# A product with the output matrix in three rounded float32 products, and four expert slots filled later

## The chip, the core and the metric

One core of one Trainium2 chip runs the whole block in one launch. The metric is the device time of an execution in microseconds; lower is better. The profile is one execution, taken by the hardware profiler. Its engines are called TensorE (PE, with weight loads as PEld), VectorE (DVE), ScalarE (ACT), GpSimd (POOL) and SyncE (SP). SyncE only issues DMAs here.

## What is computed

One layer of a streaming encoder over 512 tokens of width 1024, all in float32:

```python
h = layernorm(x, ln0)
q, k, v, z, xbc, dt, g = split(h @ w_in)
ya = window_attention(q, k, v, sinks) @ w_out_attn
ys = ssd(xbc, z, dt, ...) @ w_out_ssd
mix = (sigmoid(gA) * ya + sigmoid(gS) * ys) @ w_out     # the product that is changed
h1 = layernorm(alpha * h + mix, ln1)
moe = hier_moe(h1)        # 32 experts, d_ff 256: one of 4 groups, top 2 of its 8 experts
ple = sigmoid(h1 @ w_ple_gate + b) * (p @ w_ple)
out = layernorm(alpha * h1 + moe + ple, ln2)
```

## The kernel before

The program is written engine by engine, with hand-placed semaphores; each engine runs its own list in order. SBUF is one arena whose regions change hands. Its head is a ring of 12 slots of 2048 words in each partition (1.05 MB for the 128), into which SyncE loads the weight matrices in a fixed order, and which later holds the expert weights: a pair of experts takes six slots (gate, up and down for each half), pair 0 slots 0 to 5, pair 1 slots 6 to 11, pair 2 slots 0 to 5 again, and so on. `MOE_FREED` names, for each slot, the semaphore and the value that SyncE waits for before it loads an expert matrix there the first time.

TensorE multiplies plain fp32 operands slowly. Where it matters, the kernel splits both operands into a part rounded to fp32r (`hi`) and the rest (`lo`), and adds three products, `hi*hi + hi*lo + lo*hi` (helper `thrice`, line 875). ScalarE makes a `hi` by a copy (L1327), VectorE or GpSimd the `lo` by a subtraction (L737, L1895, L1908). The input projection and the product with `w_out_ssd` are done so. The products with `w_out_attn` (L1084), with `w_out` (L1103) and all later ones are plain fp32: one such matmul shows as two instructions in the trace.

The stretch around the change, in order:

1. `ya`: 8 output blocks of 128 columns, transposed (columns in partitions, tokens in the free dimension), into 8 PSUM banks. VectorE multiplies each with its gate into `mixT` (L1904).
2. `ys` (L875 in this stretch): 8 output blocks of 24 products each. VectorE gates a block out of PSUM (L1916, `s_ys_read`) and adds it to `mixT` (L1920, `s_mix_ready`).
3. The product with `w_out` (L1103): tokens are now in the partitions. For each of 4 token tiles and 2 halves of 512 columns, 8 matmuls over the contraction blocks go to one bank. It starts when all 8 blocks of `mixT` are there. `w_out` lies in slots 0, 1, 8, 9.
4. VectorE, for each token tile: two additions to the residual (L1929) and a layer norm (L1607 to L1613), which gives h1 (`s_h1_ready`). It also needs the rows of ln1, which GpSimd's queue loads after `ys` (L777). SyncE stores each tile of h1 to DRAM (L655, L660).
5. TensorE transposes p (L1110) and h1 (L1126) and multiplies h1 with the router (L1118). VectorE turns the logits into ranks and rows. Between, TensorE makes the first PLE gate products (L1152, L1155), which need the gate slices (four column quarters of `w_ple_gate`) and `w_ple`.
6. The first rows are gathered by GpSimd's queue, transposed (L1171), and the experts run in 16 pairs: gate and up (L1214), transposes (L1239), down (L1229). SyncE refills a pair's gate and up slots when its gate/up product is done (`s_gu_mm`), its down slots after the down product.

SyncE's list in this stretch: it waits for `ya`, loads gate slice 1, then slots 2 to 5 and 6, 7 as the `ys` product frees them; then gate slice 0, slots 10 and 11; the rows of h1 for tiles 0 to 2; after the output product `w_ple`, slots 0 and 1; the rows of tile 3; slots 8 and 9; gate slices 2 and 3 when h1 is stored and transposed.

## Time and profile before

| | |
|---|---|
| median of 3 runs | 800.39 us (799.8 to 800.94) |
| the profiled execution | 799.58 us, of it 797.8 us in the span |
| TensorE busy | 737.4 us, 92% of the span |
| VectorE, ScalarE, GpSimd busy | 406.7, 188.7, 163.0 us |
| DMA | 173.14 MB, mean 217 GB/s |

All times of the trace count from the start of the span. The page gives busy times of the engines, their course in 40 slices of 19.9 us, the chain of work that ended last, and the costliest groups of instructions. A matmul's record is longer than the step from one to the next, since matmuls are pipelined: the step is read from the starts of two instructions, or from the chain.

### The profile page before, as it was taken

To read this page: it belongs to the slowest core of one execution; us is meant where nothing else is said; L and a number is where in the kernel's file an instruction comes from. 1 tells how busy PE (TensorE), PEld (TensorE's weight loads), DVE (VectorE), ACT (ScalarE), POOL (GpSimd) and SP (SyncE) were. 2 spreads that over 40 slices of the span, in tenths; PEclk is the share of its full clock that TensorE was granted. 3 is DMA by queue.
4 is the path that set the end of the run, shared out by engine and by line. 5 is a ranking of instruction groups with operands and counts; after the bars stand their busy time and mean duration, and the time that the engine had idled before them with its cause. 6 is when DMAs were issued, how large, how long until landed. Compare 5 with 4: busy or idle time off the path is not lost.

```text
span 797.8 us, 9564 instructions
## 1 busy us (share of the span) xinstructions
PE 737.4 (92%) x3735; PEld 499.3 (63%) x3735; DVE 406.7 (51%) x743; ACT 188.7 (24%) x335; POOL 163.0 (20%) x121
## 2 busy tenths in 40 slices
PE   4999999999999999999999999999999989888672
PEld 2898788998887888747854488544554444444220
DVE  5598946775678888563216558411212021111317
ACT  3312424555322223240000060211121121111121
POOL 4924490000032222000000001411111111111242
PEclk9999999999999999999999999999999999999985
DMA  9798132311111122424268174499999999999492
GB/s 312 257 408 199 53 106 60 101 53 53 50 58 53 53 53 54 148 90 158 106 249 331 53 288 134 132 406 419 408 413 418 417 423 419 421 421 421 173 203 108
DMA packets 61815, 173.14 MB, mean 217 GB/s; under 512 B 16982, under 2 KB 39712, under 8 KB 47946
## 3 DMA queue, kind: packets, MB, share of 16 engines
q1 hardware_dynamic: 52324, 141.79, 47.1%
q0 software_dynamic: 8752, 28.59, 11.0%
q10 hardware_dynamic: 694, 2.14, 0.7%
q8 instruction: 31, 0.51, 0.3%
q14 instruction: 14, 0.11, 0.0%
HBM read 155.52 MB, written 24.67 MB: 226 GB/s over the span
## 4 chain that ended last, share of the span: by engine, by line
PE 72%; DMA 15%; DVE 8%; issue 2%; POOL 1%; ACT 1%; SPq 0%; POOLq 0%; DVEq 0%
PE psum L875 31%; PE psum L1214 10%; PE psum L1103 7%; DMA ring<-in_w_exp_up_dram 6%; PE psum L1229 5%; PE psum L1152 4%; PE psum L1084 3%; DMA ring<-in_w_in_dram 3%; DMA arena<-y_rows,rowsU 2%; PE psum L1033 2%; PE psum L1053 1%; DMA info<-row_info 1%; PE psum L983 1%; PE psum L1171 1%; PE psum L952 1%
## 5 line engine op out<-in xcount | busy, mean ns | idle before, releaser
L875 PE MATMUL psum<-ring_r 128*128 128x512 f32 (+1 forms) x832 | 215.4, 346 | 3.1 <-DVE arena_r L1638 1.7
L875 PEld LDWEIGHTS psum<-ring_r 128*128 128x128 f32 x832 | 146.2, 193 | 24.3 <-issue 3.0
L875 PE MATMUL psum<-arena_r,ring_r 128*128 128x512 f32 (+1 forms) x416 | 141.4, 377 | 0.0
L1327 ACT COPY arena<-psum 128x512 f32<-128x512 f32 (+4 forms) x104 | 57.1, 580 | 264.6 <-PE psum L1110 110.6
L1214 PE MATMUL psum<-ring,arena 128*64 128x512 f32 x512 | 112.9, 593 | 4.7 <-DMA ring<-in_w_exp_up_dram 4.7
L737 POOL TENSOR_TENSOR ring_r<-ring,ring_r 128x2048 fp32r<-128x2048 f32 x16 | 73.9, 4621 | 205.0 <-ACT ring_r L1327 205.0
L875 PEld LDWEIGHTS psum<-arena_r,ring_r 128*128 128x128 f32 x416 | 79.7, 192 | 13.7 <-issue 0.5
L1214 PEld LDWEIGHTS psum<-ring,arena 128*64 128x64 f32 x512 | 39.5, 137 | 75.4 <-issue 75.4
L1229 PE MATMUL psum<-ring,arena 128*64 128x512 f32 x256 | 61.3, 622 | 8.3 <-issue 8.3
L1152 PE MATMUL psum<-arena 128*128 128x256 f32 x256 | 63.0, 392 | 1.1 <-DVE rowsU L2061 1.1
L2092 DVE SCALAR_TENSOR_TENSOR arena<-arena,psum 128x256 f32<-128x256 f32 x16 | 9.7, 607 | 104.3 <-ACT arena L1515 104.3
L1152 PEld LDWEIGHTS psum<-arena 128*128 128x128 f32 x256 | 47.1, 192 | 18.8 <-issue 13.3
L1103 PE MATMUL psum<-ring,arena 128*128 128x512 f32 x128 | 55.2, 593 | 1.6 <-DVE arena L1920 1.6
L1327 ACT CAST ring_r<-ring 128x2048 fp32r<-128x2048 f32 x22 | 41.8, 1899 | 15.9 <-DMA ring<-in_w_in_dram 13.4
L1229 PEld LDWEIGHTS psum<-ring,arena 128*64 128x64 f32 x256 | 19.3, 143 | 40.9 <-issue 40.9
L1103 PEld LDWEIGHTS psum<-ring,arena 128*128 128x128 f32 x128 | 24.2, 190 | 32.1 <-issue 30.1
L2123 DVE COPY arena<-psum 128x512 f32<-128x512 f32 x16 | 11.1, 692 | 62.5 <-PE psum L1229 62.5
L875 PE MATMUL psum<-ring_r,arena_r 128*128 128x256 f32 (+1 forms) x144 | 41.3, 295 | 0.0
L783 POOL DMA_INDIRECT arena<-h_rows,info x14 | 14.2, 1017 | 116.1 <-PE psum L1171 106.3
L817 POOL DMA_INDIRECT y_rows<-arena,storeU x15 | 15.1, 1004 | 82.9 <-DVE arena L2123 82.6
L1515 ACT ACTIVATE arena<-psum 128x256 f32<-128x256 f32 x16 | 6.1, 383 | 105.7 <-PE psum L1214 105.7
L1084 PE MATMUL psum<-arena,ring 128*128 128x512 f32 x64 | 27.6, 592 | 0.0
(282 smaller groups left out, 908.7 us busy)
## 6 DMA issues: line engine op xcount, KB each, us to landing
ring<-in_w_exp_down_dram SPq DMA_DIRECT2D x32, 1024.0 KB, 12.4
ring<-in_w_exp_gate_dram SPq DMA_DIRECT2D x32, 1024.0 KB, 12.5
ring<-in_w_exp_up_dram SPq DMA_DIRECT2D x32, 1024.0 KB, 15.0
ring<-in_w_in_dram SPq DMA_DIRECT2D x18, 1024.0 KB, 5.2
y_rows<-arena POOLq DMA_DIRECT2D x12, 1024.0 KB, 17.0
ring<-in_w_out_ssd_dram SPq DMA_DIRECT2D x4, 1024.0 KB, 6.9
ring<-in_w_out_dram SPq DMA_DIRECT2D x4, 1024.0 KB, 4.9
arena<-in_w_ple_gate_dram SPq DMA_DIRECT2D x4, 1024.0 KB, 9.1
```

Of the source, the lines that this page charges most:

```text
L737: g.tensor_tensor(lo, ring[:, SLOT_OF[seq]], hi.bitcast(F32), ALU.subtract).then_inc(s_w_lo, 1)
L783: g.indirect_dma_start(out=xg.rearrange("p k n -> p (k n)"), out_offset=None, in_=h1_dram, in_offset=bass.IndirectOffsetOnAxis(ap=tokens, ...
L817: g.indirect_dma_start(out=y_dram, out_offset=bass.IndirectOffsetOnAxis(ap=storeU[:, p:p + 1], axis=0), in_=eout[:, p % 2, :], in_offset=N ...
L875: t = mm(o, a, b, start=(first and j == 0), stop=(last and j == 2))
L1033: t = mm(o[:, m * P:(m + 1) * P], dta[:, c, hh:hh + 1].broadcast_to([P, P]), upper, start=True, stop=True)
L1084: t = mm(o, ringN[:, s, j % 2, n * P:(n + 1) * P], yaT[:, j, :], start=(j == 0), stop=(j == 3))
L1103: t = mm(o, mixT[:, k, i * P:(i + 1) * P], ringN[:, s, k % 2, b * 512:(b + 1) * 512], start=(k == 0), stop=(k == KD - 1))
L1152: mm(ple_bank(n)[:, 0:PS], h1T[:, i, k, :], pgw[s][:, k, :], start=(k == 0), stop=(k == KD - 1))
L1214: t = mm(psum[sides[half], parity, :], xgT[parity][:, k, sides[half]], ring[:, s:s + 2, k, :], start=(k == 0), stop=(k == KD - 1))
L1229: t = mm(psum[sides[half], 4 + b, :], eactT[:, parity, k, sides[half]], ringN[:, s, k, b * 512:(b + 1) * 512], start=(k == 0), stop=(k == 1))
L1327: return nc.scalar.copy(dst, src)
L2123: v.tensor_copy(eout[:, u % 2, 512:1024], psum[:, 5, :]).then_inc(signal, 1)
```

## The change

The output product is made of three rounded products too. ScalarE makes the `hi` parts of `w_out` (`out_part`) and of the mixed activations (`mix_part`), GpSimd the rests of `w_out` in place in slots 0, 1, 8, 9 (`out_rest`), VectorE the rests of the activations in place (`mix_rest`). For token tiles 0 and 1 the contraction block is the outermost loop over four banks, and each block waits only for its own parts; tiles 2 and 3 follow bank by bank. The `hi` parts of the activations lie in slots 10 and 11, those of `w_out` in slots 2 and 3 and in the regions of `yaT`, of p's transpose and of two others, one of them that of gate slice 0. So the expert slots 2, 3, 10 and 11 can't be filled before the product ends, and `MOE_FREED` now lets only slots 4 to 7 be loaded ahead of it. SyncE's order follows: slots 4 to 7, the rows of tiles 0 and 1; after the product gate slice 0, `w_ple`, slots 0 and 1, the rows of tile 2, slots 2 and 3, the rows of tile 3, gate slice 1, slots 8 to 11, gate slices 2 and 3. Two semaphores are merged into others.

```diff
-MOE_FREED = ([("pe_mix", 2 * NT)] * 2 + [("pe_ys", KD)] * 6 + [("pe_mix", 2 * NT)] * 2 + [("ys_read", KD)] * 2)
+MOE_FREED = [("pe_ys", KD) if slot in (4, 5, 6, 7) else ("pe_mix", 2 * NT) for slot in range(12)]
...
+        mix_hi = shaped(R_RING + 10 * SLOT, "p (n t) -> p n t", True, n=KD, t=S)
+        mix_lo = mix_r[:, :].rearrange("p (n t) -> p n t", n=KD)
+        ringN_r = shaped(R_RING, "p (s k n) -> p s k n", True, s=SLOTS, k=2, n=D)
+        wo_hi = [[out_r[:, D:2 * D], out_r[:, 2 * D:3 * D]], [out_r[:, 0:D], lmat_r[:, :]]]
+        wo_hi += [[ringN_r[:, s, j] for j in range(2)] for s in (2, 3)]
... SyncE
-            sp.wait_ge(s_pe_ya, KD)
-            gate_slice(1)
-            weights_in(0, (2, 3, 4, 5))
+            weights_in(0, (4, 5))
             weights_in(1, (0, 1))
-            sp.wait_ge(s_ys_read, KD)
-            gate_slice(0)
-            weights_in(1, (4, 5))
-            for i in range(NT - 1):
+            def rows_out(i):
                 sp.wait_ge(s_h1_ready, i + 1)
                 sp.dma_start(h1_dram[i * P:(i + 1) * P], h1_words[:, i, :]).then_inc(s_h1_st, 16)
+            rows_out(0)
+            rows_out(1)
             sp.wait_ge(s_pe_mix, 2 * NT)
+            gate_slice(0)
             sp.dma_start(wple, ...)
             weights_in(0, (0, 1))
-            sp.wait_ge(s_h1_ready, NT)
-            sp.dma_start(h1_dram[3 * P:4 * P], h1_words[:, 3, :]).then_inc(s_h1_st, 16)
-            weights_in(1, (2, 3))
+            rows_out(2)
+            weights_in(0, (2, 3))
+            rows_out(3)
+            gate_slice(1)
+            weights_in(1, (2, 3, 4, 5))
...
-            gate_slice(2)
-            gate_slice(3)
+            for s in (2, 3):
+                sp.wait_ge(pgw_in[s % 2], 16)
+                gate_slice(s)
... GpSimd
+            def out_rest(s):
+                pool.wait_ge(s_w_lo, PROJ + 4 + s)
+                pool.wait_ge(s_w_hi, PROJ + 4 + s + 1)
+                w, lo = ringN[:, SLOT_OF[SEQ_WO + s]], ringN_r[:, SLOT_OF[SEQ_WO + s]]
+                link(g.tensor_tensor(lo[:, 0], w[:, 0], wo_hi[s][0].bitcast(F32), ALU.subtract))
+                g.tensor_tensor(lo[:, 1], w[:, 1], wo_hi[s][1].bitcast(F32), ALU.subtract).then_inc(s_w_lo, 1)
+            out_rest(0)
+            out_rest(1)
             pool.wait_ge(s_pe_ys, KD)
             for dst, name, landed in (... ln1_w, ln1_b, b_ple_gate ...):
                 pool.dma_start(dst, aps[name].broadcast_to([P, D])).then_inc(landed, 16)
+            out_rest(2)
+            out_rest(3)
... TensorE
-            pe.wait_ge(s_mix_ready, KD)
-            for s in range(4):
-                arrived(pe, SEQ_WO + s)
-            for i in range(NT):
-                for b in range(2):
-                    o = opened(("mix", i, b))
-                    for k in range(KD):
-                        s = SLOT_OF[SEQ_WO + k // 2]
-                        t = mm(o, mixT[:, k, i * P:(i + 1) * P], ringN[:, s, k % 2, b * 512:(b + 1) * 512],
-                               start=(k == 0), stop=(k == KD - 1))
-                    t.then_inc(s_pe_mix, 1)
+            def mixed(i, b, k):
+                ts, c = slice(i * P, (i + 1) * P), slice(b * 512, (b + 1) * 512)
+                return thrice(bank(("mix", i, b)), wo_hi[k // 2][k % 2][:, c],
+                              ringN_r[:, SLOT_OF[SEQ_WO + k // 2], k % 2, c], mix_hi[:, k, ts], mix_lo[:, k, ts],
+                              k == 0, k == KD - 1, h_stationary=True)
+            for i, b in ((0, 0), (0, 1), (1, 0), (1, 1)):
+                opened(("mix", i, b))
+            for k in range(KD):
+                pe.wait_ge(s_part_lo, NT + k + 1)
+                pe.wait_ge(s_w_lo, PROJ + 4 + k // 2 + 1)
+                for i, b in ((0, 0), (0, 1), (1, 0), (1, 1)):
+                    t = mixed(i, b, k)
+                    if k == KD - 1:
+                        t.then_inc(s_pe_mix, 1)
+            for i, b in ((2, 0), (2, 1), (3, 0), (3, 1)):
+                opened(("mix", i, b))
+                for k in range(KD):
+                    t = mixed(i, b, k)
+                t.then_inc(s_pe_mix, 1)
... ScalarE
+            def out_part(s):
+                arrived(act, SEQ_WO + s)
+                w = ringN[:, SLOT_OF[SEQ_WO + s]]
+                copy(wo_hi[s][0], w[:, 0])
+                copy(wo_hi[s][1], w[:, 1]).then_inc(s_w_hi, 1)
+            def mix_part(n):
+                act.wait_ge(s_mix_ready, n + 1)
+                act.wait_ge(s_ys_read, 6 if n < 4 else KD)
+                copy(mix_hi[:, n, :], mixT[:, n, :]).then_inc(s_part_hi, 1)
+            out_part(0)
+            out_part(1)
+            for n in range(4):
+                mix_part(n)
+            act.wait_ge(s_pe_ys, KD)
+            out_part(2)
+            mix_part(4)
+            mix_part(5)
+            out_part(3)
+            mix_part(6)
+            mix_part(7)
... VectorE
+            def mix_rest(n):
+                dve.wait_ge(s_part_hi, NT + n + 1)
+                v.tensor_tensor(mix_lo[:, n, :], mixT[:, n, :], mix_hi[:, n, :].bitcast(F32), ALU.subtract).then_inc(s_part_lo, 1)
... in the loop over the ys blocks, after block n is added to mixT
+                if n >= 6:
+                    mix_rest(2 * (n - 6))
+                    mix_rest(2 * (n - 6) + 1)
+            for n in range(4, KD):
+                mix_rest(n)
```

## Rows read from the trace of the kernel before

**Rows 1.** The page: engines' busy time; the DMA engines' busy tenths in 40 slices.

```profile
PE 737.4 (92%) x3735; PEld 499.3 (63%) x3735; DVE 406.7 (51%) x743; ACT 188.7 (24%) x335; POOL 163.0 (20%) x121
DMA  9798132311111122424268174499999999999492
```

**Rows 2.** The chain that ended last, 361 to 474 us: start us, us, what.

```profile
361.07 43.55 PE psum L875 x192
...
406.17 55.21 PE psum L1103 x128
...
461.48 0.70 DVE arena L1929
...
469.49 1.09 PE psum L1126 x8
470.58 3.51 PE psum L1118 x32
```

**Rows 3.** Timeline, VectorE, tile 0's work and tile 1's first addition: start, us.

```profile
419.50 1.46 DVE L1929 SCALAR_TENSOR_TENSOR arena<-psum,arena 128x512 f32<-128x512 f32 x2 [13.39 <-DMA arena<-in_ln_b_dram]
...
428.26 0.69 DVE L1929 SCALAR_TENSOR_TENSOR arena<-psum,arena 128x512 f32<-128x512 f32 x1
```

**Rows 4.** Timeline, TensorE, transposes after the product; brackets: idle before, its releaser.

```profile
461.20 1.04 PE L1110 MATMUL psum<-arena 128*128 128x128 f32 x8
462.08 1.91 PE L1126 MATMUL psum<-arena 128*128 128x128 f32 x16
...
469.49 1.09 PE L1126 MATMUL psum<-arena 128*128 128x128 f32 x8 [0.62 <-DVE arena L1613]
```

**Rows 5.** Busy time in a window (after POOL: PEclk, DMA share, GB/s), then TensorE's timeline.

```profile
498.00:500.00 2.00, 2.00 (x7) 1.53 (x6) 0.97 (x3) 0.00 (x0) 1.39 (x3) 0.50 0.01 1
...
496.66 3.19 PE L1152 MATMUL psum<-arena 128*128 128x256 f32 x8 [1.10 <-DVE rowsU L2061]
499.64 1.54 PE L1171 MATMUL psum<-arena 128*128 128x128 f32 x8
501.01 1.89 PE L1152 MATMUL psum<-arena 128*128 128x256 f32 x8
502.74 1.03 PE L1155 MATMUL psum<-arena 128*128 128x256 f32 x4
```

**Rows 6.** Timeline, 68 to 79 us: GpSimd's rests beside VectorE's two-input instructions.

```profile
68.41 9.66 POOL L737 TENSOR_TENSOR ring_r<-ring,ring_r 128x2048 fp32r<-128x2048 f32 x2 [12.68 <-ACT ring_r L1327]
...
68.97 4.61 DVE L1692 SCALAR_TENSOR_TENSOR arena<-arena 128x512 f32<-128x512 f32 x1 [1.64 <-ACT arena L1385]
...
76.81 1.81 DVE L1692 SCALAR_TENSOR_TENSOR arena<-arena 128x512 f32<-128x512 f32 x1
```

**Rows 7.** The chain, one z product of 48 rounded products of 256 columns.

```profile
131.80 5.75 PE psum L875 x48
```

**Rows 8.** Timeline, ScalarE, VectorE and GpSimd: what the new parts resemble.

```profile
347.36 3.88 ACT L1327 CAST arena_r<-arena 128x1024 fp32r<-128x1024 f32 x4
...
399.98 0.69 DVE L1920 TENSOR_TENSOR arena<-arena 128x512 f32<-128x512 f32 x1
...
405.97 0.53 POOL L777 DMA_DIRECT2D arena<-in_b_ple_gate_dram  x1
```

**Rows 9.** Timeline, SyncE's issues: the first refill, for pair 2.

```profile
510.83 0.34 SPq L644 DMA_DIRECT2D ring<-in_w_exp_gate_dram  x1
```

**Rows 10.** Windows: after the product, gate slices, weights; the last three columns as in rows 5.

```profile
461.40:486.00 24.60, 1.00 0.82 303
...
481.00:485.00 4.00, 4.00 (x23) 3.61 (x22) 3.47 (x16) 0.73 (x3) 0.00 (x0) 1.00 0.98 314
...
540.00:560.00 20.00, 20.00 (x99) 9.23 (x95) 3.24 (x6) 2.73 (x6) 2.03 (x2) 1.00 1.01 419
```

**Rows 11.** Timeline, TensorE, the first gate/up product and a late one.

```profile
503.70 7.09 PE L1214 MATMUL psum<-ring,arena 128*64 128x512 f32 x32
...
727.43 7.09 PE L1214 MATMUL psum<-ring,arena 128*64 128x512 f32 x32 [2.59 <-DMA ring<-in_w_exp_up_dram]
```

More of the change, by code:

```diff
@@ L262, in block_kernel @@
                 pass
+            with nc.sbuf_tensor("to_x_r", [P, 12544], F32R):
+                with nc.sbuf_tensor("mix_r", [P, 4096], F32R) as mix_r:
+                    with nc.sbuf_tensor("out_r", [P, 3 * D], F32R) as out_r:
+                        with nc.sbuf_tensor("to_l_r", [P, 4096], F32R):
+                            with nc.sbuf_tensor("lmat_r", [P, D], F32R) as lmat_r:
+                                pass
             with nc.sbuf_tensor("arena_r", [P, ARENA], F32R) as arena_r:
@@ L539, in block_kernel @@
         s_yT_read = sem("yT_read")
-        s_yT_hi = sem("yT_hi")
-        s_yT_lo = sem("yT_lo")
+        s_part_hi = sem("part_hi")
+        s_part_lo = sem("part_lo")
         s_y_act = sem("y_act")
@@ L773, in _ @@
             pool.wait_ge(s_pe_yT, NT)
-            pool.dma_start(p_in, p_v).then_inc(s_p_in, 16)
+            pool.dma_start(p_in, p_v).then_inc(s_small_in, 16)
+            def out_rest(s):
[6 more added lines that the diff above has]
+            out_rest(1)
             pool.wait_ge(s_pe_ys, KD)
-            for dst, name, landed in ((A1w, "ln1_w", s_ln_in), (A1b, "ln1_b", s_ln_in), (bple, "b_ple_gate", s_bple_in)):
+            for dst, name, landed in ((A1w, "ln1_w", s_ln_in), (A1b, "ln1_b", s_ln_in), (bple, "b_ple_gate", s_small_in)):
                 pool.dma_start(dst, aps[name].broadcast_to([P, D])).then_inc(landed, 16)
+            out_rest(2)
+            out_rest(3)
             def rows_fetched(p):
@@ L1085, in _ @@
                 t.then_inc(s_pe_ya, 1)
-            pe.wait_ge(s_yT_lo, NT)
+            pe.wait_ge(s_part_lo, NT)
             for n in range(KD):
@@ L2005, in ple_out @@
                 dve.wait_ge(s_base_ready, seen(s_base_ready))
-            dve.wait_ge(s_bple_in, 16)
+            dve.wait_ge(s_small_in, 16 * 8)
             ple_sum(0)
```

12 lines of the change are left out of this document (5 added, 7 removed).

## Prediction

> **What bounds the kernel now.** I read the page first: TensorE is busy 92% of the span, in 40 slices almost evenly, while the DMA engines are full over a long stretch only in slices 27 to 37 [rows 1]. A high busy share says little by itself, so the next view is the chain of work that ended last. From 361 us on it runs through TensorE without a gap: the SSD output product (192 products, 43.55 us), a short VectorE step, then the product with the output matrix, L1103, 55.21 us [rows 2]. Behind that stands the last token tile's layer norm on VectorE (from 461.48), its transposes, which start at 469.49, and the router [rows 2]. So every microsecond that the last tile's h1 comes earlier is a microsecond for the router, the first gathered rows and the first gate/up product at 503.70, whose end lets SyncE fetch pair 2's weights at 510.83 [rows 9, 11]. From there the DMA queue is full (share 1.01 [rows 10]) and TensorE waits for weights late in the stage (2.59 us at 727 [rows 11]). The expert stage thus begins when that first refill is issued and shifts as a block with it. The question is how much earlier the last h1 comes and whether the stage finds its weights there.
>
> **The product itself.** Before: 64 plain fp32 matmuls of 512 columns, each issued as two instructions, 55.21 / 128 = 431 ns apiece [rows 2]. After: 64 x 3 = 192 rounded products. The same helper gives the pace: 43.55 / 192 = 0.2268 us with 512 columns [rows 2], and with the activations stationary, as here, 48 products of 256 columns took 5.75 us, 120 ns each [rows 7], so weight loads don't bind even at half the columns. Twice 120 ns is the upper bound (46.1 us), 0.2268 my value: 192 x 0.2268 = 43.55 us, 11.7 us less.
>
> **Its start.** Before, it waits for the last block of the mixed activations: 1.54 us between the end of the SSD product (404.62) and 406.17 [rows 2]. Now contraction block 0 needs only its own parts. VectorE ends block 6 at 400.67 (399.98 + 0.69 [rows 8]) and then makes rests 0 and 1, two instructions of 0.69 us: ready at 402.1. The output weights 0 and 1 are split during the SSD product, where ScalarE is idle. So the product starts at 404.63, 1.5 us earlier, and would end at 448.2 instead of 461.38: 13.2 us on TensorE.
>
> **Does it run without a stall?** Each contraction block feeds four banks with three products, 12 x 0.2268 = 2.72 us, so block k starts at 404.63 + 2.72k: block 3 at 412.8, block 4 at 415.5, block 6 at 421.0, block 7 at 423.7. ScalarE after 404.65: four 128x1024 casts (0.97 each, 3.88 for four [rows 8]) and four 128x512 casts, about 0.55 each: weight part 2 at 406.7, blocks 4 and 5 at 407.8, part 3 at 409.8, blocks 6 and 7 at 410.9. GpSimd first issues its three row DMAs (the last at 405.97, 0.53 us [rows 8]), then makes the weights' rests, two instructions of 128x1024 each. Its 128x2048 subtraction takes 4.6 us (two in a row 9.66 [rows 6]), so a half is 2.3: weight rest 2 stands at about 411.6, rest 3 at 416.5. VectorE has eight instructions here (block 7's two, rests 2 to 7), 0.72 us each with issue.
> These two engines get in each other's way. In the rows, a 128x512 instruction of VectorE with two SBUF inputs, normally 0.69 us, took 4.61 us beside a GpSimd subtraction, yet it ended between the two GpSimd instructions, and the next one took 1.81 [rows 6]. So VectorE waits out one GpSimd instruction and then gets its turn. Taking turns with four halves of 2.3 us, rests 3 to 7 end at about 409.9, 412.9, 415.9, 418.9 and 419.6, and weight rest 3 at 418.2. All are before 412.8, 415.5, 418.2, 421.0 and 423.7: no stall, with 2 to 3 us to spare. That is the cover; without it the cost is rival 2. (The Trainium skill, GPSIMD Engine Reference, section Specifications, says that GpSimd shares its SBUF interfaces with VectorE and contends with instructions that have two SBUF inputs. The rows agree: 4.61 for 0.69 us. By that sentence alone the time is open between no stall and rival 2.)
>
> **What VectorE makes of it.** Contraction-outermost order has a price: bank (0,0) is complete only after 87 products, at 404.63 + 19.73 = 424.4, and banks of tiles 0 and 1 follow within 2.1 us. Tiles 2 and 3 end at 437.3 and 448.2. One tile of VectorE work, two residual additions and a layer norm, takes 428.26 - 419.50 = 8.76 us [rows 3]. Tile 0 starts at 424.4 (in the trace of before it started at 419.50, held by the layer norm's rows, not by TensorE [rows 3]; fewer loads are queued beside those rows now, so they land by about 419.5 again, 5 us early). Then each tile waits for VectorE, not for TensorE: 424.4 + 4 x 8.76 = 459.45. TensorE alone would give 448.2 + 0.05 + 8.0 (461.48 to 469.49 [rows 2]) = 456.25. So VectorE becomes the bound of this stage: the last h1 at 459.45 instead of 469.45, a gain of **10.0 us** and not 13.2. Bounds: 13.2 if tile 0 could start as early as before, 5.9 with rival 2's stall.
>
> **What TensorE's clock takes back.** TensorE ends the product at 448.2, makes p's transposes, h1's tiles 0 and 1, the router of tile 0 (after VectorE has read bank 6, at 451.4), tile 2, and the router of tile 1: 8 + 24 transposes and 32 router matmuls at 0.11 us, until about 456.0. Then it stands still until 459.5, 3.4 us, where before it stood 0.62 [rows 4]. In the trace, after 16 router-like matmuls of 2 columns and 1.1 us idle, the granted clock was 0.50 at 498 to 500, the lower of its two levels (1.2 for 2.4 GHz) [rows 5]. There eight matmuls of L1152 took 2.98 us to the next start (496.66 to 499.64) against 1.73 (501.01 to 502.74), and eight transposes 1.37 (499.64 to 501.01) against 0.88 (461.20 to 462.08 [rows 4]): one visit cost 1.75 us. I expect such a visit at 458 to 463, and there the 8 transposes and 32 router matmuls (4.6 us, 469.49 to 474.09 [rows 2]) lie on the path. Bounds: nothing, if the clock stays up as it did over the same work before; 4.6, if all of it runs at half speed. I take **1.5 us**, near the visit that the rows show. (The Trainium skill, TensorE: Matmul & The Clock Gate, section Why this matters for your kernels, warns that pauses between bursts bring the low clock back. It speaks against this change, which lengthens one pause; by it the sum is 1.5 us worse than without.)
>
> **The refills.** Eight expert slots now wait for the product (four did), and so do all four gate slices and w_ple: 13 loads of 1.05 MB and two 0.52 MB row stores behind 448.2, 14.7 MB, against some 7.9 before. The queue in order: gate slice 0, w_ple, slots 0 and 1, rows 2 (h1 at 450.7), slots 2 and 3, rows 3 (459.4), gate slice 1, slots 8 to 11, gate slices 2 and 3. Weights move at 419 GB/s, 2.5 us each, gate slices at 314 in the nearest stretch, 3.3 us [rows 10]. So slice 0 and w_ple land by 455 (needed at 464 when the PLE products start), slots 0 to 3 by 466 (needed at 493.7), row store 3 by 468 (gather at 481), gate slice 1 by 471 (needed at 487), slots 8 to 11 by 481 (needed at 510), the rest by 487. The next refill is due at 510.83 - 10 + 1.5 = 502.3 [rows 9], so 15 us of empty queue cover it. Before, the empty queue of the product's second half was wasted. I cost this part at nothing; without that cover each microsecond of backlog beyond 502.3 costs one. p's and b_ple's semaphore merge into one that is complete by 423: nothing. The row stores 0 and 1 stand ahead of SyncE's wait for the product and are issued at 433.2 and 441.9: nothing.
>
> **Sum.** 799.58 (the profiled execution) - 10.0 + 1.5 = 791.1. The median of the runs is 0.8 above that execution, so 791.9.
>
> **Rivals.**
> 1. The clock stays up. For: over the same transposes and router work before it did [rows 4]. Against: the pause is 3.4 us now. Gives 800.4 - 10.0 = 790.4.
> 2. The port stalls the product. If GpSimd keeps the port through its four halves, rest 3 ends only at 406.9 + 4 x 2.3 + 0.7 = 416.8, 4.0 us after block 3 is due, and bank (0,0), hence all tiles, come 4.0 us later: 795.9 with the clock's visit, 794.4 without. For: a VectorE instruction of 0.69 us took 4.61. Against: it got its turn between two GpSimd instructions [rows 6].
> 3. Slower: the refill queue is the bound. Place: SyncE's queue behind 448.2. The gate slices and the long queue would have to keep pair 2's refill waiting. It decides once the 14.7 MB take longer than 54.1 us (to 502.3), under 272 GB/s; it is slower than before under 236 GB/s (62.4 us). At 210 GB/s, 70 us, it gives 791.9 + 15.9 = 807.8. For: half the loads moved there. Against: the mean of 461.4 to 486 was 303 GB/s with the queue partly empty [rows 10].
> 4. The change doesn't do what it says: the new waits keep the product from starting before block 7 is split. Then 1.5 to 8 us of the start are lost: 793 to 800.
>
> **How the numbers follow.** Forecast with one visit of the low clock 0.55; rival 1 0.20; rival 2 0.12; rival 3 0.04; rival 4 and what I have not seen 0.09. Rival 1 lies at 790.4 with the spread of runs of 1.1 around it; a second weak stretch at 485 to 490, where the clock fell before too, may or may not be hit (1.75 us either way). So 788.8 to 796.5 holds the forecast, rival 1 and rival 2, 0.8 after allowing for mis-sized terms. A measurement of this kernel can tell about 0.2%, 1.6 us, from no change. Faster by more: 0.93; within: 0.03; slower: 0.04.
>
> **What would show each step.** The 192 products in 43.5 us, from 404.6 to 448.2, without an idle before blocks 3, 4 and 6; a gap at block 3 is rival 2. The first residual addition at 424.4, row stores at 433.2, 441.9, 450.7 and 459.4, VectorE without a pause between; if the tiles are apart by more than 8.76, the 10.0 is wrong. TensorE idle of about 3.4 us before the last eight transposes, and a granted clock under 1 just after; with 1.00 there rival 1 holds. The queue empty from about 487 until the refill at 502; if it is full there, rival 3. What would make the forecast wrong most easily is a smaller shift of the refill than of h1.

## The result, and the profile after

| | kernel before | kernel after |
|---|---|---|
| median | 800.54 us (799.80 to 801.17, 5 runs) | 796.83 us (795.95 to 797.18, 5 runs) |
| ratio | | 0.9948, 95% interval 0.9934 to 0.9963 |
| the profiled execution | 799.58 us, span 797.8 | 796.83 us, span 795.0 |

The change makes the kernel faster by 3.7 us of the medians, 2.8 us between the two profiled executions. The forecast was 8.6 us (791.9, range 788.8 to 796.5), so the time lies just outside it, and more than half of the gain is missing. I followed it stage by stage. First the chain of work that ended last (start us, us, what) of the kernel after; it answers to [rows 2]:

```profile
360.59 63.27 PE psum L902 x279
423.98 0.70 DVE arena L2001
...
432.80 0.70 DVE arena L2001
...
441.65 0.70 DVE arena L2001
...
450.42 0.70 DVE arena L2001
```

The SSD product and the new product (both now L902) are one unbroken piece on TensorE. From 423.98 on the chain is VectorE's: the residual additions of the four token tiles (L2001) start 8.8 us apart. The timelines of GpSimd (weights' rests) and VectorE (activations' rests) beside the product:

```profile
406.32 2.78 POOL L795 TENSOR_TENSOR ring_r<-ring,ring_r 128x1024 fp32r<-128x1024 f32 x1 [0.27 <-ACT ring_r L1365]
...
414.79 2.72 POOL L796 TENSOR_TENSOR ring_r<-ring,ring_r 128x1024 fp32r<-128x1024 f32 x1
...
405.55 12.51 DVE L1957 TENSOR_TENSOR mix_r<-arena,ring_r 128x512 fp32r<-128x512 f32 x6
```

And TensorE behind the product (in brackets: idle before, and its releaser), against [rows 4] and [rows 5]:

```profile
451.16 1.98 PE L1156 MATMUL psum<-arena 128*128 128x36 f32 x16 [0.89 <-DVE arena L2001]
452.97 1.42 PE L1164 MATMUL psum<-arena 128*128 128x128 f32 x8
454.18 3.46 PE L1156 MATMUL psum<-arena 128*128 128x36 f32 x16
459.14 1.97 PE L1164 MATMUL psum<-arena 128*128 128x128 f32 x8 [1.50 <-DVE arena L1676]
460.91 6.88 PE L1156 MATMUL psum<-arena 128*128 128x36 f32 x32
467.59 5.18 PE L1190 MATMUL psum<-arena 128*128 128x256 f32 x16
...
491.93 3.75 PE L1190 MATMUL psum<-arena 128*128 128x256 f32 x8 [1.20 <-DVE rowsU L2133]
495.47 1.92 PE L1209 MATMUL psum<-arena 128*128 128x128 f32 x8
...
500.23 7.09 PE L1252 MATMUL psum<-ring,arena 128*64 128x512 f32 x32
```

The last h1 is there 10.35 us earlier (459.14 against 469.49 [rows 4]). But the 8 transposes and 32 router matmuls behind it, 4.42 us before to the start of the first PLE product (469.49 to 473.91), now take 8.45. The windows show why (window, its length, busy time of PE, PEld, DVE, ACT and POOL, then granted clock, DMA share, GB/s):

```profile
447.00:453.00 6.00, 5.11 (x44) 4.71 (x42) 5.83 (x6) 3.01 (x4) 0.00 (x0) 1.00 0.61 190
453.00:454.00 1.00, 1.00 (x10) 1.00 (x10) 0.86 (x5) 0.00 (x0) 0.00 (x0) 0.77 1.02 370
454.00:470.00 16.00, 14.50 (x64) 13.91 (x63) 6.55 (x20) 9.64 (x6) 0.00 (x0) 0.50 1.00 396
...
471.00:491.00 20.00, 19.73 (x111) 17.78 (x109) 16.51 (x61) 1.14 (x4) 1.39 (x1) 1.00 0.94 348
491.00:498.00 7.00, 6.07 (x19) 5.15 (x20) 3.00 (x11) 1.16 (x3) 4.02 (x4) 0.51 0.02 6
```

The granted clock is at its lower level (0.50, that is 1.2 of 2.4 GHz) from about 453.5 to 470.4, some 17 us, where before it stood at 1.00 over all of this work (461 to 475). It fell not in the pause that I had looked at but before it, after a wait of 0.89 us that began at 450.3, while router matmuls and transposes ran. So the later pause is only 1.50 us: the slow work fills the rest. A second visit, 491 to 498, is longer than that of before (497 to 501 [rows 5]).

The gain at each station, start before minus start after, from the timelines:

| station | before | after | gain |
|---|---|---|---|
| last h1's transposes | 469.49 | 459.14 | 10.35 |
| first PLE gate product | 473.91 | 467.59 | 6.3 |
| ranks | 482.63 | 477.79 | 4.8 |
| PLE product after `rowsU` | 496.66 | 491.93 | 4.7 |
| first gate/up product | 503.70 | 500.23 | 3.5 |
| first refill issued | 510.83 | 507.36 | 3.5 |
| last gate/up product but one | 727.43 | 722.63 | 4.8 |
| end of the span | 797.8 | 795.0 | 2.8 |

6.9 of the 10.35 us are gone before the first refill. In the experts 1.3 come back, and the gate/up product of the last pair but one (the 15th of 16), 7.09 us before [rows 11], gives 1.7 away at a low clock:

```profile
722.63 8.78 PE L1252 MATMUL psum<-ring,arena 128*64 128x512 f32 x32 [2.13 <-DMA ring<-in_w_exp_up_dram]
```

### The profile page after: what moved, and what is told of

Read it like the earlier page. It is cut to its first block, busy times and chain, and to the rows that moved or that the text cites. A ratio compares the mean times of both kernels' runs of the same rounds, so it can differ in the third digit from the quotient of the medians.

```text
span 795.0 us, 9744 instructions
## 1 busy us (share of the span) xinstructions
PE 736.1 (93%) x3799; PEld 519.1 (65%) x3799; DVE 422.8 (53%) x751; ACT 201.2 (25%) x351; POOL 183.9 (23%) x129
## 4 chain that ended last, share of the span: by engine, by line
PE 75%; DMA 11%; DVE 9%; issue 2%; POOL 1%; ACT 1%; SPq 0%; DVEq 0%; POOLq 0%
PE psum L902 34%; PE psum L1252 12%; PE psum L1190 6%; DMA ring<-in_w_exp_up_dram 6%; PE psum L1267 5%; PE psum L1111 3%; DMA ring<-in_w_in_dram 3%; PE psum L1060 2%; PE psum L1080 1%; PE psum L1193 1%; PE psum L1209 1%; PE psum L1010 1%; DMA arena<-y_rows,rowsU 1%; DVE arena L1676 1%; PE psum L979 1%
## 5 line engine op out<-in xcount | busy, mean ns | idle before, releaser
L902 PE MATMUL psum<-ring_r 128*128 128x512 f32 (+1 forms) x928 | 246.6, 350 | 4.1 <-DVE arena_r L1701 1.7
L902 PEld LDWEIGHTS psum<-ring_r 128*128 128x128 f32 x928 | 163.3, 191 | 29.0 <-issue 4.0
L902 PE MATMUL psum<-arena_r,ring_r 128*128 128x512 f32 (+1 forms) x416 | 140.9, 376 | 0.0
L902 PEld LDWEIGHTS psum<-arena_r,ring_r 128*128 128x128 f32 x416 | 79.2, 190 | 13.7 <-issue 0.5
L1190 PE MATMUL psum<-arena 128*128 128x256 f32 x256 | 65.4, 403 | 1.2 <-DVE rowsU L2133 1.2
L1190 PEld LDWEIGHTS psum<-arena 128*128 128x128 f32 x256 | 49.1, 200 | 19.5 <-issue 12.2
L1365 ACT CAST ring_r<-ring 128x2048 fp32r<-128x2048 f32 (+1 forms) x26 | 45.8, 1768 | 24.0 <-DMA ring<-in_w_in_dram 13.3
L902 PE MATMUL psum<-ring_r,arena_r 128*128 128x256 f32 (+1 forms) x144 | 41.3, 295 | 0.0
L1492 ACT ACTIVATE ring<-psum,arena 128x512 f32<-128x512 f32 x16 | 11.0, 689 | 65.0 <-PE psum L902 65.0
L902 PEld LDWEIGHTS psum<-ring_r,arena_r 128*128 128x128 f32 (+1 forms) x144 | 26.0, 181 | 2.1
```

What stands on the lines that cost most here:

```text
L902: t = mm(o, a, b, start=(first and j == 0), stop=(last and j == 2))
L1190: mm(ple_bank(n)[:, 0:PS], h1T[:, i, k, :], pgw[s][:, k, :], start=(k == 0), stop=(k == KD - 1))
L1365: return nc.scalar.copy(dst, src)
L1492: A(gact[:, n, b, :], bank(("g", g)), ACT.Tanh, scale=0.5, bias=b_gate[:, 8 * b + n:8 * b + n + 1]).then_inc(s_g_read, 1)
```

## The experiments

The theories: (A) the low clock takes the gain, and it follows from TensorE's pauses; (B) something else slows TensorE behind 450, above all the loads that now run there (share 1.00 in the window of 454 to 470, 0.82 before [rows 10]); (C) SyncE's longer queue delays the first refill. To fill a pause I gave TensorE a **filler**: plain fp32 matmuls of 512 columns into a free bank, whose result nobody reads. All else in these kernels computes what it did.

### Both pauses filled

```diff
+            def filler(n):
+                for _ in range(n):
+                    mm(psum[:, 3, 0:4 * P], ident, h1T[:, 0, 0:4, :], start=True, stop=True)
             for i in range(NT):
+                if i == 3:
+                    filler(3)
                 pe.wait_ge(s_h1_ready, i + 1)
...
                 if i == 1:
+                    pe.wait_ge(s_h1T_read, 1)
+                    filler(1)
                     logits = opened("rt", NT * 36)
```

> The changed kernel, with TensorE's two pauses behind the output product filled by plain fp32 products of 512 columns whose result nobody reads (one before the router of tile 0, three before the transposes of tile 3; nothing is left out). Theory A, the low clock: the missing 5 to 6 us went to TensorE's granted clock, which was 0.50 from 453.6 to 470.3, brought on by thin work (transposes, router matmuls of 36 columns) with pauses between. Then the granted clock stays at 1.00 there, the last 8 transposes and 32 router matmuls take 4.6 us instead of 8.65, the first gate/up product starts at about 494.5 instead of 500.3, and the run takes 791 to 792 us. Theory B, traffic: the transposes and router matmuls are slow since the DMA queue is full beside them (share 1.0 from 451 to 485, where before it was partly empty). Then they still take 8.6 us and the run takes 797 us.

Measured: 792.69 us (791.91 to 795.90, 4 runs), 0.9902 (0.987 to 0.9935) of the kernel before. TensorE's timeline at the last tile, and two windows:

```profile
459.35 1.09 PE L1171 MATMUL psum<-arena 128*128 128x128 f32 x8 [0.57 <-DVE arena L1685]
460.28 3.92 PE L1156 MATMUL psum<-arena 128*128 128x36 f32 x32
```

```profile
456.00:464.00 8.00, 7.43 (x48) 5.65 (x48) 3.26 (x2) 3.52 (x3) 0.00 (x0) 0.97 1.00 391
464.00:470.00 6.00, 6.00 (x22) 5.10 (x23) 5.00 (x21) 5.07 (x3) 0.00 (x0) 0.76 1.01 405
```

With the DMA engines as full as before (share 1.00) the same transposes and router matmuls take 4.7 us instead of 8.5. Matmuls that do nothing useful make the kernel some 4 us faster: theory B falls, and that the low clock takes the gain stands. The clock still fell at the end of the router (0.76 from 464 to 470), later and shorter, though no pause since the product was longer than 0.57 us; so pauses are not all that brings it down.

### One pause at a time

first_filled has only `filler(1)` ahead of the first router block, with its wait. second_filled has only the other, with 2 matmuls:

```diff
             for i in range(NT):
+                if i == 3:
+                    pe.wait_ge(s_h1T_read, 1)
+                    filler(2)
```

> Only the first pause (0.89 us at 450, before the router of tile 0) is filled, with one product of 512 columns. Theory A with the first pause as the trigger: the clock stays up through the routers of tiles 0 and 1 (they end at 456.0, not 457.6), and falls, if at all, in the pause of 3.1 us behind them; then one visit of a few us, 792 to 795 us. If only the long pause mattered, the fall at 453.6 stays where it is and the run takes 796.8.

> Only the second pause is filled, with two products of 512 columns (at the low clock they take 3.4 us and hold up tile 3's transposes by 1.9 us). Theory A: the clock falls at 453.6 as it did, the filling brings it back at about 461, and the router of tiles 2 and 3 runs at full speed: 8 transposes and 32 router matmuls in 5 to 6 us, the run at 794 to 796. Theory B: 8.6 us as before and the delay on top, 798 to 799 us.

first_filled: 797.31 us (795.46 to 798.84, 7 runs), 0.9952 (0.9937 to 0.9967), no gain, where I had expected 792 to 795. The first pause is gone, both early router blocks run at full clock, and then the long pause comes, now 3.23 us, and does the same harm:

```profile
454.32 1.87 PE L1156 MATMUL psum<-arena 128*128 128x36 f32 x16
459.43 1.97 PE L1169 MATMUL psum<-arena 128*128 128x128 f32 x8 [3.23 <-DVE arena L1683]
461.19 6.88 PE L1156 MATMUL psum<-arena 128*128 128x36 f32 x32
```

second_filled: 790.65 us (789.68 and 791.63), 0.9868 (0.9838 to 0.9899). In its profile the clock is 1.00 from 451 to 470, although the first pause of 0.94 us is still there; I had expected the fall at 453.6 to stay, and 794 to 796 us. With two runs I didn't trust it, and ran it again beside the changed kernel itself:

> The fillers of second_filled, once more and with more runs: only two stood behind its 790.65. If that was the cost of the clock alone, the median is 790 to 792 again, and the long pause is the one that counts. If its two runs were lucky ones, in which the clock stayed up after the first pause too, then part of the runs lies at 794 to 797 now, and both pauses count.

> The changed kernel once more, unedited, beside the two kernels of this group, so that they are compared on one chip. Clock theory: 796 to 797.5, at 0.995 of the kernel before, with the granted clock at 0.50 behind 454 again. If the low clock there was an accident of the first profile, the profile shows 1.00 between 454 and 471 and the time is 791 to 793.

second_again: 790.51 us (788.74 to 796.57, 5 runs), 0.9861 (0.9832 to 0.9891). after_again: 796.36 us (795.07 to 798.23, 9 runs), 0.9949 (0.9931 to 0.9967). Both medians repeat. The one run of second_again at 796.57, the others being at 788.74 to 791.00, is the profiled one, and TensorE's timeline and a window show what differs:

```profile
451.20 1.97 PE L1156 MATMUL psum<-arena 128*128 128x36 f32 x16 [0.95 <-DVE arena L2009]
...
454.52 3.47 PE L1156 MATMUL psum<-arena 128*128 128x36 f32 x16
457.80 3.76 PE L1163 MATMUL psum<-arena 128*128 128x512 f32 x4
461.35 1.92 PE L1172 MATMUL psum<-arena 128*128 128x128 f32 x8
```

```profile
454.00:460.00 6.00, 6.00 (x23) 4.95 (x22) 4.80 (x11) 1.01 (x1) 0.00 (x0) 0.50 1.00 395
```

Here the clock fell after the first pause, of 0.95 us, in a kernel in which it did not after 0.94 us in another execution. So the two pauses are two chances to lose the clock. The long one (3.2 us) took it in the execution seen with the first filled; the short one takes it in some executions and not in others. Up to 455 second_filled and the changed kernel do the same work, and only one of seven runs of second_filled and second_again has the longer time. So in many executions of the changed kernel it may be the long pause that costs, though its two profiles both show the fall behind the short one; with one profiled execution per run, how often each does it stays open.

### The same short pause in the kernel before

```diff
                 if i == 1:
                     logits = opened("rt", NT * 36)
+                    pe.wait_ge(s_h1T_read, 2)
```

> The kernel before, where the router of tile 0 also waits until ScalarE has copied h1's tile 1 out of PSUM: a pause of about 1.1 us at 464 instead of 0.3, which by itself holds up nothing by more than 0.2 us. Theory A: the granted clock falls behind it (as it did in the changed kernel behind a pause of 0.89 us), the transposes and the router of tiles 2 and 3 take up to 8.6 us instead of 4.6, and the run takes 803 to 806 us. Theory B: 800.5 to 801 us, the clock at 1.00.

The router of tile 0 waits for one more ScalarE copy; the pause before it is 1.19 us, 0.32 in before. Measured: 804.44 us (797.54 to 808.95, 10 runs), 1.0049 (1.0018 to 1.0081). The runs fall into two groups: four of 797.5 to 800.3 us with a mean granted clock of 0.979 to 0.983, five of 805.3 to 809.0 with 0.967 to 0.970, and one between (803.5, 0.975). With no other change than a pause of about one microsecond in front of thin matmuls, the old kernel thus took 5 to 8.5 us more in half of its executions. By the mean clocks (0.979 against 0.968 over some 797 us) that is some 18 us more at half speed, an estimate, as long as the visit in after. The profiled execution is one of the shorter ones (1.00 from 451 to 505), so where the clock fell in the others isn't seen: that it fell behind this pause is argued from the edit, and what decides between the two groups stays open.

### A third filler, and useful work instead

all_filled is both_filled with one more in the pause at 487. useful_filled has that too, and in the long pause, instead of two of the three fillers, the first half of the gate product of PLE unit 0.

```diff
+            filler(1)
             ple_half(EARLY, 0)
             rows_turned_in(0)
```

```diff
                 if i == 3:
-                    filler(3)
+                    opened(("pl", 0))
+                    ple_half(0, 0)
+                    filler(1)
```

> The changed kernel with both pauses filled as in both_filled, and one more product of 512 columns whose result nobody reads, behind the 16 router-like products of 2 columns at 488 us, in front of the pause for the rows (the pause where the clock was low at 491 to 498 in the changed kernel). Clock theory: TensorE's granted clock is 1.00 from 404 us until the experts; the gate/up product of pair 0 starts at 493 to 494 in every run; 790 to 791.5 us median, with less spread than both_filled. Rival (what is left of the gap to 790.4 is not the clock's): as both_filled, 792.7.

> As all_filled, but the second pause is filled with work that is needed anyway: the first four gate matmuls of PLE unit 0 (1.7 us), and one product whose result nobody reads. The PLE work behind the router is then 1.7 us shorter, and TensorE's first PLE stretch (8.7 us) was what the ranks product waited for. If TensorE is the bound between the router and the ranks product, the run is up to 0.6 us faster than all_filled, since VectorE's selection (8.0 us from the logits) takes over as the bound; if VectorE is the bound already, the same.

all_filled: 793.02 us (791.40 to 795.93, 6 runs), 0.9906 (0.9885 to 0.9927), against an expectation of 790 to 791.5. The visit at 490 is gone (1.00 from 485 to 505), the one at 464 to 467 is as in both_filled, and the median didn't move. useful_filled: 791.86 us (791.18 to 792.29, 4 runs), 0.989 (0.9869 to 0.9912), clock 1.00 from 404 to 505 in its profile. Its intervals overlap with those of the others, so "better than both_filled" isn't shown; that it beats the changed kernel by some 5 us is. But its first gate/up product started at 491.69, 8.5 us earlier than in the profile of after. Again something behind it takes back three of them.

### The clock's old visit in the kernel before

```diff
+            filler(1)
             ple_half(EARLY, 0)
             rows_turned_in(0)
```

> The kernel before with one filler behind the second turned block of rowsU, ahead of the PLE product at 496.66, where its trace shows the granted clock at 0.50. Clock theory: this visit (1.75 us) goes, the first gate/up product starts at about 502.3 instead of 503.70, 798.5 to 800, and 485 to 505 shows 1.00. If a visit costs the end nothing, since the stage behind it waits for weights, 800.5 as before. Neither reaches the changed kernel's 796.8: if it did, the gain of the change would have been the clock's all along.

That is the product at 496.66 [rows 5]. Measured: 800.41 us (799.87 to 803.23, 10 runs), 1.0 (0.9986 to 1.0015). The visit is gone (1.00 from 485 to 505) and the first gate/up product starts at 501.08 instead of 503.70 (0.9 us of it was there before: the last tile's transposes start at 468.55 in this execution, not at 469.49), yet the time is that of before. So the gain of the change is not the clock's, and a microsecond ahead of the first refill isn't one at the end. In this kernel's profile 0.8 us of the 2.6 are lost between the refill and the 15th gate/up product and 1.7 in that product, at a low clock (8.78 us). For the first of these losses, here are the timelines of SyncE, GpSimd and TensorE in after_again, whose second visit happened not to come, so that its first refill is 2.8 us earlier than in the profile of after:

```profile
504.56 0.34 SPq L654 DMA_DIRECT2D ring<-in_w_exp_gate_dram  x1
505.69 1.49 POOL L829 DMA_DIRECT2D info<-row_info  x1 [1.43 <-DMA row_info<-token_info,rowsU]
517.37 1.06 POOL L810 DMA_INDIRECT arena<-h_rows,info  x1 [10.18 <-DMA info<-row_info]
525.59 1.97 PE L1209 MATMUL psum<-arena 128*128 128x128 f32 x8 [3.09 <-DMA arena<-h_rows,info]
```

Pair 2's rows are gathered by a list (`info`) that GpSimd loads when its eight scattered writes have landed. If the 1 MB weight loads are issued first, the small load takes over 10 us beside them, and TensorE waits 3.09 us for the rows, at a low clock afterwards (1.97 us for eight transposes). The third gate/up product comes 20.8 us after the second one instead of 16.06. In the profile of after the list was issued 1.46 us ahead of the refill:

```profile
505.90 1.49 POOL L829 DMA_DIRECT2D info<-row_info  x1 [1.43 <-DMA row_info<-token_info,rowsU]
514.00 1.05 POOL L810 DMA_INDIRECT arena<-h_rows,info  x1 [6.61 <-DMA info<-row_info]
```

### Hold the refill back?

Against useful_again, the unchanged useful_filled, on the same chip:

```diff
             for p in range(2, PAIRS):
                 sp.wait_ge(s_gu_mm, p - 1)
+                if p == 2:
+                    sp.wait_ge(s_w_row, 16 * 2 * NT)        # info_issued
+                    sp.wait_ge(s_w_row, 16 * 2 * NT + 16)   # info_landed, in its place
                 weights_in(p, (0, 1, 3, 4))
```

> The kernel useful_filled once more, as the partner of the next two on the same chip. 791 to 792.5. In its first profile the pair's gate/up products started at 491.69, 507.80 and 528.29: 16.11 and then 20.49 apart, 4.4 over the steady pitch of 16.06, with TensorE waiting 2.79 us for the gathered rows before the turn at 519.54. The same is expected here: 4 to 5 over the pitch.

> useful_filled, and SyncE holds back pair 2's first refill until the eight scattered row descriptions have landed, which is when GpSimd issues the load of the row list. It moves the refill from 498.8 to about 500, beside the list's load and not 1.1 us ahead of it. If the early refill is what delays the list: TensorE's wait before the turn at 519 falls from 2.8 to about 1 (0.82 to 1.12 us in the profiles in which the two were issued within 0.3 us of each other), the transposes stay at full clock, and the time falls by 2 to 3 us to 789 to 790. If the list is late by itself: same wait, and 792 to 793, since the refill is only later.

> useful_filled, and SyncE holds back pair 2's first refill until the row list has landed, so that the list meets an empty queue. If traffic delays the list: it lands in 3 to 8 us instead of 11.5, no wait before the turn, the third gate/up product 16.1 us behind the second one, 4.4 us earlier. Against that the refill comes at 503 to 507 instead of 498.8, and its weights are needed at 524: 6.3 MB at 419 GB/s are 15 us, so up to 1 to 3 us of a wait for weights may take its place, and the late wait for weights (2.57 us at 717) may grow. Forecast 788.5 to 790.5. If the list is late by itself: 793 to 797.

useful_again 791.64 us (789.19 to 794.65), info_issued 792.85 (789.41 to 796.39), info_landed 793.10 (792.67 to 794.93), 4 runs each; ratios 0.9896 (0.9871 to 0.9922), 0.9886 (0.984 to 0.9931) and 0.99 (0.9884 to 0.9917). The medians miss my expectation of a gain of 2 to 3 us in both. The runs of info_issued lie in two pairs, at 789.41 and 789.57 as expected and at 796.13 and 796.39; the profiled one is of the latter, so what the former did isn't seen. In info_landed the mechanism is there: the list is seen landed 5.5 us after its issue (500.01 to 505.54), TensorE has no wait for it, and the third product comes 16.05 us after the second:

```profile
505.54 1.05 POOL L812 DMA_INDIRECT arena<-h_rows,info  x1 [4.04 <-DMA info<-row_info]
...
507.86 7.04 PE L1268 MATMUL psum<-ring,arena 128*64 128x512 f32 x32
...
523.91 7.04 PE L1268 MATMUL psum<-ring,arena 128*64 128x512 f32 x32
```

But by the 15th gate/up product, 196.0 us later (191.3 in useful_again), what was won is lost again, and the medians show neither a gain nor a loss. All profiles together, us; "lead" is how long the list's load was issued ahead of the first refill (minus: behind it), "wait" TensorE's wait for the rows gathered with it, "stage" the time from the first refill to the 15th gate/up product:

| profile | first refill | lead | wait | 15th gate/up | stage |
|---|---|---|---|---|---|
| info_landed | 504.84 | +4.8 | none | 719.91 | 215.1 |
| after | 507.36 | +1.5 | none | 722.63 | 215.3 |
| refill_late (below) | 500.79 | +0.7 | none | 716.87 | 216.1 |
| useful_again | 500.81 | +0.6 | none | 717.18 | 216.4 |
| bank_by_bank (below) | 509.05 | +0.5 | none | 725.12 | 216.1 |
| before | 510.83 | +0.3 | 0.82 | 727.43 | 216.6 |
| second_filled | 500.26 | +0.1 | 1.12 | 717.07 | 216.8 |
| first_filled | 506.57 | +0.2 | 0.78 | 723.36 | 216.8 |
| before_pause | 509.19 | -1.1 | 1.64 | 725.90 | 216.7 |
| second_again | 505.25 | +0.2 | 1.24 | 722.29 | 217.0 |
| before_filled | 508.21 | -1.1 | 1.84 | 725.57 | 217.4 |
| both_filled | 500.94 | -1.1 | 2.16 | 719.43 | 218.5 |
| all_filled | 500.76 | -1.1 | 2.33 | 719.28 | 218.5 |
| useful_filled | 498.82 | -1.1 | 2.79 | 717.74 | 218.9 |
| after_again | 504.56 | -1.1 | 3.09 | 724.07 | 219.5 |
| info_issued | 501.46 | -0.2 | 2.92 | 721.04 | 219.6 |

Where TensorE doesn't wait for the list, the stage takes 215.1 to 216.4 us from the first refill, with a DMA share of 1.00 all the way (505 to 720 in after), and up to 3 us more when the list comes late. One kernel shows both: 218.9 us with the wait (useful_filled), 216.4 without (useful_again). Holding the refill back for the list saves the wait and pays for it in the refill. To gain, the list would have to come earlier. That wasn't tried.

useful_again also says how little a short visit of the low clock can cost. Its profiled execution, at 789.19 us the fastest of this kernel, lost the clock twice ahead of the refill (0.58 from 463 to 467, 0.50 from 487 to 490), in useful_filled it stayed at 1.00 and the run took 791.18. TensorE's timeline of useful_again:

```profile
459.90 4.10 PE L1156 MATMUL psum<-arena 128*128 128x36 f32 x32
463.80 3.23 PE L1180 MATMUL psum<-arena 128*128 128x256 f32 x8
...
486.64 3.55 PE L1180 MATMUL psum<-arena 128*128 128x256 f32 x8 [0.46 <-DVE rowsU L2147]
```

The refill came 2.0 us later, so the list was ahead of it and TensorE did not wait. Since the product TensorE had paused for 0.56 us at most before the first fall and for 0.46 us just before the second; in info_issued the clock fell at 463 too, with no pause over 0.65 us. In before it stayed up behind 0.62 us [rows 4]. What brings the clock down in such cases these runs don't show.

### The refill queue, and the loop order

refill_late is both_filled with a wait for the ranks' product (473.2), so that slots 8 to 11 and gate slices 2 and 3 come later:

```diff
             gate_slice(1)
+            sp.wait_ge(s_pe_rk, 1)
             weights_in(1, (2, 3, 4, 5))
```

> both_filled with the loads of slots 8 to 11 and gate slices 2 and 3 held back until the ranks product (474 us, about 12 us later than they are issued in both_filled). The cover that the prediction names is the queue's empty stretch from 487 to the first refill at about 501. If it is there, these 6.3 MB (15 us) land by 491 and the time is that of both_filled, 792.7. If the refill queue is the bound already (rival 3), each us of delay shows, and the run takes 800 us or more.

793.38 us (791.93 and 794.84), 0.9908 (0.9878 to 0.9938), the time of both_filled. The queue is busy until later (DMA share 0.77 from 490 to 495, 0.08 in the profile of after), and the refill comes at 500.79, as in both_filled (500.94). Two things cancel in this: the clock stayed at 1.00 from 451 to 470, and TensorE waited 1.52 us for the first gathered rows at 490.05, which it doesn't in both_filled. So holding the loads back by some 12 us cost about 1.5 us and not 12. Theory C falls: the refill still follows the first gate/up product at once, and in after the queue stands nearly empty before it.

bank_by_bank is the changed kernel with the new product in the old order:

```diff
-            for i, b in ((0, 0), (0, 1), (1, 0), (1, 1)):
-                opened(("mix", i, b))
-            for k in range(KD):
-                ...
+            for i in range(NT):
+                for b in range(2):
+                    opened(("mix", i, b))
+                    for k in range(KD):
+                        if i == b == 0:
+                            pe.wait_ge(s_part_lo, NT + k + 1)
+                            pe.wait_ge(s_w_lo, PROJ + 4 + k // 2 + 1)
+                        t = mixed(i, b, k)
+                    t.then_inc(s_pe_mix, 1)
```

> The changed kernel with the output product bank by bank for all four token tiles (contraction innermost), the waits for the parts inside bank (0,0). Prediction's working: bank (0,0) then ends only when the last rests stand (block 7 at about 418), so the product ends at 418 + 0.7 + 7 x 5.44 = 457 instead of 447.5, VectorE is no longer its bound, and the last h1 comes at 457 + 8 = 465 instead of 459.1. If the rests were not what holds the product (rival), it ends at 448 and the last h1 comes at 456. The time is 802 in the first case if the clock falls as in the changed kernel, 796 if not.

TensorE's timeline shows three waits. 800.03 us (798.14 to 800.75, 8 runs), 0.999 (0.9975 to 1.0006): no gain at all from three rounded products in this order.

```profile
406.17 0.50 PE L902 MATMUL psum<-out_r,ring_r 128*128 128x512 f32 x1 [0.81 <-DVE mix_r L1952]
411.84 0.70 PE L902 MATMUL psum<-ring_r 128*128 128x512 f32 x2 [4.03 <-POOL ring_r L796]
417.37 1.19 PE L902 MATMUL psum<-ring_r 128*128 128x512 f32 x2 [3.27 <-POOL ring_r L796]
```

The first bank wants all weight rests at once: 8.1 us of waits, part of the product at a low clock (0.88 on average from 404 to 447), the product's end at 459.48 instead of 447.49 and the last h1 at 467.75 instead of 459.14. I had expected 457 and 465: the low clock, 0.54 from 412 to 420 around waits of 4.03 and 3.27 us, was not in that sum. The order with the contraction outermost is worth 8.6 us of h1.

## Why the prediction was right and wrong

- **The product, its start, no stall:** right. The chain shows 63.27 us for both products; the new one runs from 403.96 to 447.49, 43.5 us, without an idle. (It all lies 0.5 us earlier than before, since `ya` started at 360.59 and not at 361.07.) GpSimd's halves took 2.72 to 2.78 us, not 2.3: of the four earlier ones (367.8 to 378.0) three took 2.40 to 2.41 us, and 2.73 the one beside which VectorE ran an addition with two SBUF inputs (372.30). So the halves are slower beside VectorE. Six rests took 12.51 us, four of them behind a GpSimd instruction each, as the taking of turns said. The last was ready at 418.06, 4.9 us before its block (403.96 + 7 x 2.72 = 423.0): rivals 2 and 4 have no case.
- **VectorE becomes the bound:** right. Residual additions at 423.98, 432.80, 441.65 and 450.42 (forecast 424.4 and steps of 8.76), last h1 at 459.1, 10.35 us earlier where I said 10.0; 0.5 of it is the earlier start of the whole stretch.
- **The refills:** right. The queue was empty from about 490 until the refill at 507.36; I said 487. Rival 3 has no case, by refill_late too.
- **What the clock takes back:** this is the step that failed, in its size and in its place. I counted one visit, 1.5 us, with 0 and 4.6 as bounds. In the profile of after it is 4.0 on the transposes and router of the last tile (nearly my upper bound of 4.6, all of it at half speed), 1.5 on the PLE product behind, 1.3 more than before in the visit at 491 to 498, and 1.7 in the 15th gate/up product. The place: I named the pause of 3.4 us ahead of the last tile and passed over my own sentence that the router of tile 0 has to wait for VectorE until 451.4. That pause, 0.89 us, came first in both profiles of this kernel. (With it filled, the long pause did the same harm: first_filled. So the size is what failed in either case.) And I took a visit's length from one of some 4 us under wide PLE matmuls [rows 5], while here transposes and matmuls of 36 columns followed the fall and it lasted some 17 us. The pauses that preceded a fall around the router were of 0.89 (after), 0.92 (after_again), 0.95 (second_again) and 3.23 us (first_filled), but in both_filled, info_issued and useful_again of no more than 0.65. (The Trainium skill, TensorE: Matmul & The Clock Gate, section A second HAM failure mode: psum-queue depth-cycling, tells of a bf16 kernel in which frequent micro-idles between groups of matmuls made the clock go back and forth between its two levels. If that holds for fp32 work too, short pauses count as well as a long one; the traces agree in part, with a fall behind 0.95 us in second_again and none behind 0.94 in second_filled. I had weighed only the section on long pauses.)
- **"The expert stage shifts as a block with the first refill":** right within about 2 us, and that was not in the sum. Earlier refills can overtake the row list: in after_again the refill was 6.3 us earlier than before, 2.9 us of them were lost in the stage. In the profile of after the list led, and the clock had taken the time instead. As I read it, the two losses stand in for each other: the profiled executions with and without the long second visit took 796.83 and 797.40 us.
- **Rival 1** (clock stays up behind the product, 790.4) is what the kernel would be without that: second_filled, 790.65 and 790.51. The forecast of 10.0 us for the product was good by the h1 itself; that the total fits so well is partly luck. Rival 1 keeps the old visit of 1.75 us, and without it the sum is 788.6, but useful_filled, whose clock stayed at 1.00 up to the experts, took 791.86; some 2.5 us of the difference are the late list's (a stage of 218.9 us against 216.4). I gave 0.55 to a mild visit and priced no heavy one, though I named its bound; with 4.6 and one more visit of 1.75 in the sum, the time would have been 796.7, which leaves out the 1.3 won and the 1.7 lost behind the refill.

## What to carry to other kernels

Where a faster product hands the bound to another engine, TensorE gets pauses it didn't have; look at each wait between the product and the next wide matmul, also those under a microsecond, and price the case in which the thin work behind (transposes, routers) all runs at half speed. Wide matmuls in the pause made that case rarer and shorter here; they did not rule it out. Hoist useful matmuls into it, or let TensorE multiply for nothing. And when a stage is said to shift as a block, list the small transfers that share the queue at its start, since the large ones that come earlier may overtake them.

## What the runs showed of the hardware

- Behind a pause of 0.89 to 0.95 us, followed by transposes and matmuls of 36 columns, the granted clock fell to 0.50 in the profiles of after, after_again and second_again; behind 0.94 us at the same place (second_filled) and behind 1.19 (before_pause) it stayed at 1.00. It also fell with no pause over 0.65 us, at the end of 32 such matmuls (both_filled, info_issued, useful_again).
- At the lower level, 8 transposes and 32 matmuls of 36 columns took 8.45 us (after), at the upper one 4.42 (before and second_filled); eight transposes 1.97 against 1.09.
- Behind a late wait for weights of 2.1 to 2.9 us the low clock comes in some profiles and not in others: the 32 matmuls behind it took 8.78 us in after (2.13 us of wait), 7.09 in before (2.59) and after_again (2.48). Where the wait was 1.20 us or less (refill_late, bank_by_bank), they took 7.09.
- A small load issued 1.1 us behind four weight loads of 1 MB was seen by the waiting engine 11.7 us after its issue (505.69 to 517.37), with no weight load ahead of it 5.5 us (info_landed).
- GpSimd's 128x1024 subtraction took 2.72 to 2.78 us beside VectorE's two-input instructions; three earlier ones in the same execution, without such a one beside them, took 2.40 to 2.41.
